# A mixture-of-experts layer on one core: expert rows stored each to a row of its own and summed when the turns end

## What is computed

```python
# T = 768 tokens in layer 0, 512 in layer 1; D = 1024; 64 experts, 8 of them per token
idx = lax.top_k(sel, TOP_K)[1]
wts = jnp.take_along_axis(scores, idx, axis=1)
wts = wts / jnp.sum(wts, axis=-1, keepdims=True) * ROUTED_SCALE
...
def expert_block(...):          # 128 rows of one expert
    xb = h_pad[tok]
    return (jax.nn.silu(xb @ w_eg[e]) * (xb @ w_eu[e])) @ w_ed[e]
routed = jnp.zeros((T + 1, D), h.dtype).at[row_tok].add(y * row_w[:, None])[:T]
shared = (jax.nn.silu(h @ w_sg) * (h @ w_su)) @ w_sd
x = x + gt2 * (routed + shared)
```

## Time and profile before

| | us |
|---|---|
| median of three runs | 3712.47 |
| lowest and highest run | 3701.37, 3768.01 |
| the profiled execution | 3699.51 |
| its span, first to last instruction | 3697.7 |
| layer 0: end of the loop's matmuls to TensorE's next full work | 2049.5 to 2107.8 |
| layer 1: end of the loop's matmuls to the end of the span | 3650 to 3697.7 |

### The profile page before, as it was taken

The page is one execution under the profiler, slowest core; times in us unless marked ns, Lnnn a source line. Parts: engine busy times, 40 slices in busy tenths (PEclk is TensorE's granted clock), DMA queues, the critical chain, the costliest instruction groups (busy, mean ns, idle before and its releaser), DMA issues.

```text
span 3697.7 us, 42657 instructions
## 1 busy us (share of the span) xinstructions
PE 3436.1 (93%) x13496; PEld 2137.5 (58%) x13496; DVE 975.2 (26%) x1798; ACT 755.5 (20%) x1337; POOL 631.0 (17%) x767
## 2 busy tenths in 40 slices
PE   7999999999986999999999499999997799999994
PEld 3468877899653444445444248877764344444442
DVE  2243242122242111111111335233324111111113
ACT  2343242112111111111111235232211111111111
POOL 0000300000023222222222200110003222222222
PEclk9979999999978999999999799979997899999997
DMA  6210211344215999999998510102222899999995
GB/s 241 81 58 7 72 40 58 120 139 146 104 66 218 345 354 348 354 354 355 350 359 297 166 47 1 49 18 69 90 100 71 320 350 343 340 352 344 340 342 149
DMA packets 223706, 735.36 MB, mean 199 GB/s; under 512 B 47842, under 2 KB 96388, under 8 KB 169428
## 3 DMA queue, kind: packets, MB, share of 16 engines
q1 hardware_dynamic: 176356, 601.80, 43.8%
q0 software_dynamic: 47248, 132.13, 14.4%
HBM read 669.89 MB, written 98.31 MB: 208 GB/s over the span
## 4 chain that ended last, share of the span: by engine, by line
PE 90%; DVE 3%; DMA 2%; issue 1%; ACT 1%; POOL 1%; SPq 0%; another core or an unknown queue 0%; POOLq 0%; DVEq 0%; ACTq 0%
PE ps L765 26%; PE ps L792 13%; PE ps L743 8%; PE ps L714 7%; PE ps L721 5%; PE ps L722 5%; PE ps L723 5%; PE ps L899 5%; PE ps L918 4%; PE ps L992 4%; PE ps L820 1%; PE ps L1009 1%; POOL slot_list L1745 1%; PE ps L1004 1%; PE ps L876 1%
## 5 line engine op out<-in xcount | busy, mean ns | idle before, releaser
L765 PE MATMUL ps<-ring,region_q 128*128 128x512 f32 x1120 | 492.2, 592 | 0.0
L1775 POOL DMA_INDIRECT acc<-region_q,idx_out x141 | 226.3, 1605 | 1060.1 <-DVE region_q L1421 1004.0
L743 PEld LDWEIGHTS ps<-con,region_c 128*128 128x128 f32 x1766 | 243.7, 171 | 201.3 <-issue 154.9
L765 PEld LDWEIGHTS ps<-ring,region_q 128*128 128x128 f32 x1120 | 207.9, 191 | 234.4 <-issue 234.4
L743 PE MATMUL ps<-con,region_c 128*128 128x128 f32 x1766 | 281.0, 288 | 51.3 <-DMA region_c<-h_rows,idx_in 28.7
L1057 ACT ACTIVATE region_q<-ps 128x512 f32<-128x512 f32 (+2 forms) x308 | 194.0, 630 | 629.6 <-PE ps L792 416.3
L723 PE MATMUL ps<-region_x_split,ring_split 128*128 128x384 f32 (+2 forms) x800 | 284.4, 356 | 0.0
L765 PE MATMUL ps<-region_k,region_q 128*128 128x512 f32 x576 | 258.2, 602 | 1.7 <-DVE region_q L1389 1.7
L792 PE MATMUL ps<-ring,region_c 128*128 128x512 f32 x560 | 252.0, 593 | 1.0 <-DVE region_c L1401 1.0
L765 PE MATMUL ps<-region_v,region_q 128*128 128x512 f32 x560 | 246.3, 593 | 0.7 <-DVE region_q L1389 0.7
L1073 ACT ACTIVATE region_c<-ps 128x256 f32<-128x256 f32 x141 | 54.1, 384 | 912.7 <-PE ps L765 912.7
(11 more groups left out here) (279 smaller groups left out, 5075.4 us busy)
## 6 DMA issues: line engine op xcount, KB each, us to landing
ring<-in_w_exp_gate SPq DMA_DIRECT2D x70, 1024.0 KB
ring<-in_w_exp_up SPq DMA_DIRECT2D x70, 1024.0 KB
ring<-in_w_exp_down SPq DMA_DIRECT2D x70, 1024.0 KB
ring<-in_w_mod SPq DMA_DIRECT2D x24, 2048.0 KB, 8.1
region_k<-in_w_exp_gate SPq DMA_DIRECT2D x36, 1024.0 KB
region_k<-in_w_exp_up SPq DMA_DIRECT2D x36, 1024.0 KB
region_k<-in_w_exp_down SPq DMA_DIRECT2D x36, 1024.0 KB, 10.4
region_v<-in_w_exp_gate SPq DMA_DIRECT2D x35, 1024.0 KB
```

The costliest lines, as they stand in the source:

```text
L743: last = nc.tensor.transpose(ps[0:t.shape[1], at:at + t.shape[0]], t, ident[0:t.shape[0], 0:t.shape[0]])
L765: last = mm(m_gu[s], xgT[:, s, k, :], wgu[w][:, :, k, :], start=k == 0, stop=k == DK - 1)
L1775: pool.indirect_dma_start(ACC[s], bass.IndirectOffsetOnAxis(ap=idx_out[:, s:s + 1], axis=0), yb[:, s, :], None, compute_op=ALU.add).then_i ...
```

## The change

- Each of a token's eight expert rows gets a place of its own in HBM: `y_rows` has 768 x 8 rows of 1024 numbers, and the list's entry (8 x token + choice) is the row number. The scatter is a plain write; entries past the end are left out by a bounds check.
- The shifted list goes to a tile `rows` of its own, used by the gather; the unshifted `slots` serves the scatter.
- The accumulators, their zeroing, the zero rows of `h_rows` and the stores of the shared expert go. The shared rows (`sd`) are drained by VectorE: times gt2, then added to XT ahead of the loop.
- Behind the loop SP loads, per tile of 128 tokens, a token's eight rows to one partition: rows 0 to 3 as `half_a` (2 MB, a third of `ring`), rows 4 to 7 as `half_b` (2 MB in K, VY or HT). Three tiles fit; the load of tile i waits until tile i - 3 is summed.
- VectorE adds half a pairwise (128x2048, 128x1024). TensorE adds half b by multiplying each row block with the identity and accumulating in PSUM, 8 matmuls of 128x512 per tile. VectorE adds the PSUM sum, multiplies by gt2 and adds to XT. GpSimd adds nothing any more.
- Only the latent tiles are saved to `x_saved` (4 of 6).

```diff
-                add("sd", l, u, drain="act", panel=("shd", l))
+                add("sd", l, u, drain="dve", panel=("shd", l))
...
-    ACC = [nc.dram_tensor(f"acc{i}", [TOK + P, D], F32, kind="Internal").ap() for i in range(2)]
+    Y8 = nc.dram_tensor("y_rows", [TOK * TOPK, D], F32, kind="Internal").ap()
...
+        half_a = [ring[:, 4096 * i:4096 * i + 4096] for i in range(3)]
+        half_b = [w[:, 0:4096] for w in (K, VY, HT)]
...
                 for i, t in enumerate(A):
-                    for a in range(2):
-                        sp.dma_start(comb[i][:, a, :], ACC[a][t * P:t * P + P, :]).then_inc(s_comb[i], 16)
+                    y = Y8[t * P * TOPK:(t + 1) * P * TOPK, :].rearrange("(p j) d -> p (j d)", p=P)
+                    if i >= 3:
+                        sp.wait_ge(b_summed, before + i - 2)
+                        sp.wait_ge(combined, before + i - 2)
+                    sp.dma_start(half_a[i % 3], y[:, 0:4096]).then_inc(s_half_a[i], 16)
+                    sp.dma_start(half_b[i % 3], y[:, 4096:8192]).then_inc(s_half_b[i], 16)
+                    if i >= 3:
+                        save(i - 3)
...
+                    for i in range(len(active(l))):
+                        pe.wait_ge(s_half_b[i], 16 * (l + 1))
+                        if i >= 2:
+                            pe.wait_ge(combined, NT * l + i - 1)
+                        for half in range(2):
+                            for j in range(TOPK // 2):
+                                at = D * j + 512 * half
+                                last = mm(slot[i % 2][:, 512 * half:512 * half + 512], ident, half_b[i % 3][:, at:at + 512],
+                                          start=j == 0, stop=j == TOPK // 2 - 1)
+                        last.then_inc(b_summed, 1)
...
                 for i, t in enumerate(A):
-                    a = comb[i]
-                    dve.wait_ge(summed, i + 1 + (NT if l else 0))
-                    link(tt(a[:, 0, :], a[:, 0, :], BC["gt2", 0 if t >= CT else 1], ALU.mult))
-                    tt(XT[:, t, :], XT[:, t, :], a[:, 0, :], ALU.add).then_inc(combined, 1)
+                    a = half_a[i % 3]
+                    dve.wait_ge(s_half_a[i], 16 * (l + 1))
+                    link(tt(a[:, 0:2 * D], a[:, 0:2 * D], a[:, 2 * D:4 * D], ALU.add))
+                    link(tt(a[:, 0:D], a[:, 0:D], a[:, D:2 * D], ALU.add))
+                    dve.wait_ge(b_summed, NT * l + i + 1)
+                    link(tt(a[:, 0:D], a[:, 0:D], slot[i % 2], ALU.add))
+                    link(tt(a[:, 0:D], a[:, 0:D], BC["gt2", 0 if t >= CT else 1], ALU.mult))
+                    tt(XT[:, t, :], XT[:, t, :], a[:, 0:D], ALU.add).then_inc(combined, 1)
...
+                elif kind == "sd":
...
+                    tt(yb[:, n % 2, :], ps, BC["gt2", 0 if t >= CT else 1], ALU.mult).then_inc(drained["dve"], 1)
+                    dve.wait_ge(drained["dve"], job.count)
+                    link(tt(XT[:, t, :], XT[:, t, :], yb[:, n % 2, :], ALU.add))
...
-                    pool.indirect_dma_start(ACC[s], bass.IndirectOffsetOnAxis(ap=idx_out[:, s:s + 1], axis=0),
-                                            yb[:, s, :], None, compute_op=ALU.add).then_inc(sl[f"scat{s}"], 16)
+                    pool.indirect_dma_start(Y8, bass.IndirectOffsetOnAxis(ap=idx_out[:, s:s + 1], axis=0), yb[:, s, :], None,
+                                            bounds_check=TOK * TOPK - 1, oob_is_err=False).then_inc(sl[f"scat{s}"], 16)
...
-                for i, t in enumerate(A):
-                    a = comb[i]
-                    pool.wait_ge(s_comb[i], 32 * (l + 1))
-                    gp.tensor_tensor(a[:, 0, :], a[:, 0, :], a[:, 1, :], ALU.add).then_inc(summed, 1)
```

More of the change, by code:

```diff
@@ L219, in build @@
           choice, nobody, out):
-    H = nc.dram_tensor("h_rows", [TOK + P, HROW], F32, kind="Internal").ap()
-    ACC = [nc.dram_tensor(f"acc{i}", [TOK + P, D], F32, kind="Internal").ap() for i in range(2)]
+    H = nc.dram_tensor("h_rows", [TOK, HROW], F32, kind="Internal").ap()
+    Y8 = nc.dram_tensor("y_rows", [TOK * TOPK, D], F32, kind="Internal").ap()
     LISTS = [nc.dram_tensor(f"slot_list{l}", [P * LISTN, 1], I32, kind="Internal").ap() for l in range(DEPTH)]
+    SPARE = [nc.dram_tensor(f"spare{s}", [P, 1], I32, kind="Internal").ap() for s in range(2)]
     XS = nc.dram_tensor("x_saved", [TOK, D], F32, kind="Internal").ap()
@@ L354, in build @@
         slots = C[:, 3712:3712 + LISTN].bitcast(I32)
+        rows = C[:, 4096:4096 + LISTN].bitcast(I32)
         xgT = Q[:, 0:2048].rearrange("p (a k s) -> p a k s", a=2, k=DK)
@@ L1248, in _ @@
                     last = copy(hTb[:, n % 2, :], ps[:, 0:DE])
-                elif kind == "sd":
-                    n = active(l).index(a[1])
-                    if n >= 2:
-                        act.wait_ge(s_sh[n % 2], store_no(l, n) - 16)
-                    last = copy(yb[:, n % 2, :], ps)
                 elif kind == "moe":
@@ L1403, in moe @@
                 dve.wait_ge(sl["list_in"], 16)
-                ts(slots, slots, 3, None, ALU.logical_shift_right).then_inc(sl["slots_ready"], 1)
+                ts(rows, slots, 3, None, ALU.logical_shift_right).then_inc(sl["slots_ready"], 1)
                 dve.sem_inc(sl["y_b"], 1)
@@ L1455, in _ @@
             vec.tensor_copy(trib[:], cst("tri"))
-            vec.memset(zero[:], 0.0).then_inc(s_zero, 1)
             for job in jobs:
@@ L1631, in _ @@
                     last = tt(hb[:, n % 2, :], s1[:, n % 2, :], ps[:, DE:2 * DE], ALU.mult)
+                elif kind == "sd":
+                    t = a[1]
+                    n = active(l).index(t)
+                    if n == 0:
+                        for s in range(2 if l < DEPTH - 1 else 1):
+                            after(dve, "bc", l, "gt2", s)
+                    tt(yb[:, n % 2, :], ps, BC["gt2", 0 if t >= CT else 1], ALU.mult).then_inc(drained["dve"], 1)
+                    dve.wait_ge(drained["dve"], job.count)
+                    link(tt(XT[:, t, :], XT[:, t, :], yb[:, n % 2, :], ALU.add))
                 elif kind == "pos":
@@ L1784, in _ @@
                     gather(w, w)
+                if l:
+                    for i in range(NT):
+                        pool.wait_ge(s_half_a[i], 16 * l)
+                        pool.wait_ge(s_half_b[i], 16 * l)
                 for s in range(2):
-                    pool.wait_ge(s_sh[s], store_no(l, len(A) - 2 + s))
-                pool.wait_ge(s_acc1, 16 * (NT + (len(A) if l else 0)))
-                for s in range(2):
-                    pool.dma_start(ACC[s][TOK:TOK + P, :].rearrange("p (a n) -> p a n", a=4), zr).then_inc(sl[f"scat{s}"], 16)
+                    pool.dma_start(SPARE[s], place[:, 0:1]).then_inc(sl[f"scat{s}"], 16)
                 with pool.Fori(0, max_turns(l) // UNROLL) as m:
```

42 lines of the change are left out of this document (16 added, 26 removed).

## The result

The changed kernel took 3826.1 us as the median of four runs (3768.9 to 3893.9), the kernel before beside it 3740.2 us (3701.4 to 3797.6). The ratio is **1.018, interval 1.014 to 1.022**. It compares only the runs of each kernel that lie within 1.5% of its fastest one. Two repeats with more runs gave 1.027 (1.019 to 1.036) and 1.024 (1.015 to 1.034). The change makes the kernel slower by about 2%; on which side of 2% it lies, the three intervals leave open. The median of the first measurement lies above my range, the ratio where the sum had put it.

A forecast was written before the change was run, and what follows sets the result against it. TensorE was taken to pace the loops; the loads behind them cost: 41.7 + 27.4 - 2 x 1.6 - 0.6 + 0.7 = +66.0 us on 3699.5, so 3765.5, with a median allowance 3770 us; range 3748 to 3808 us.

The forecast's parts named there:

- The turns: Expert loops: plain writes replace 141 scatters with addition, TensorE sets the turn of 11.42 us, so 0 change.
- Rivals D and E: D: plain scatter lengthens turns, 3911 us, 4%; E: fewer bytes shorten turns, 3630 us, 4%; at 1 us per turn.
- The last scatter, -1.6 us per layer: End of each loop: plain scatter lands in 4.5 us instead of 6.13, -1.6 us per layer, between -3.1 and 0.
- The streams: Loads behind the loops: 25.17 MB and 16.78 MB at 415 GB/s; stages +41.7 us and +27.4 us.
- rival B: Loads behind the loops run slower, at 346 GB/s; sum +86, 3790 us; 18%.
- The rule weighed: Loads behind the loops: the skill's 358 GB/s per core would make the sum 16 us more; the trace shows 412 to 421.
- The last tile's sum, 8.4 us: Behind the stream: TensorE adds the last tile's half b, 8.4 us, the middle of 6.87 and 9.96 us.
- The lead of 6 us: Loads behind layer 0's loop: tile 4's load may start about 2096, before 2102, so the stream stays full.
- rival C: Behind the loops: TensorE at half clock sets the tiles, 13.3 us each; sum +101, 3805 us; 8%.
- ScalarE's backlog: After the last addition: ScalarE no longer comes to the following code with a backlog, -0.6 us.
- the shared part: Ahead of the loops: VectorE's shared-expert work delays layer 1's list shift, +0.7 us, between 0 and 1.4.
- Rival F: Start of the loops shifts by 10 us either way, to 3760 or 3780 us; 6%.

The follow-up runs named there:

- experiment 5: Kernel before with a plain write in place of the addition in the scatter; 3732.3 us, ratio 1.015 (1.009 to 1.020).
- experiment 4: Changed kernel with GpSimd's loop alone cut from 28 and 24 rounds to 19 and 17; 3774.3 us, ratio 1.023 (1.017 to 1.028).
- experiment 3: Changed kernel with one 128x128 matmul per tile in place of the eight that sum half b; 3757.1 us, ratio 1.016 (1.010 to 1.023).
- experiment 2: Changed kernel loading only half of each token's row data behind the loops, additions and matmuls keeping their shapes; 3769.2 us, ratio 1.022.
- experiment 6: Kernel before with VectorE gating and adding the shared rows ahead of the loop, both accumulators zeroed; 3683.6 us against 3692.0, ratio 1.000 (0.997 to 1.003).
- the combined version: Kernel before with VectorE adding the shared expert ahead of the loop and the two accumulators without GpSimd; 3719.3 us, ratio 1.005; again 3719.2 us, 1.003.
- the changed kernel's third and second: Profiles of the changed kernel run again unedited; third measurement 3813.3 us, ratio 1.024 (1.015 to 1.034), second 3817.7 us, 1.027 (1.019 to 1.036).

## Why the prediction was right, and where it was not

**The turns: right.** 871.8 us with 870.07 us of TensorE, as before, though share and bytes of the queues fell. The plain scatters landed in 9.3 us in the median, not in the 6 of the last one, and still well inside the two turns that cover them. Rivals D and E ask for turns of another length; experiment 5 refutes E a second time.

**The last scatter, -1.6 us per layer: the step failed.** I took 4.5 us to landing; it is 2.82 (experiment 4), just under the 3 to 6 us that I had named as the sign. By that the gain should have been 3.3 us. But the step never asked what was late next. The first load came 0.8 us later in layer 0 and 2.1 earlier in layer 1, since GpSimd's empty loop rounds, hidden behind 6.13 us of landing before, now stand on the path, and its drain behind them is of no fixed length (2.70 us before, 3.92 after in layer 0; 3.83 and 2.12 in layer 1). Sum of both layers -1.3 us instead of -3.2.

**The streams: right that the bytes set them; that the length agrees in layer 0 is luck.** First load's issue to the last byte's signal: predicted 63.0 us, measured 63.4, at 413 to 436 GB/s. In layer 1 predicted 43.9, measured 43.4 (3830.05 to 3873.43). That takes out rival B. But I took 415 GB/s, and tiles come at 428: by that layer 0 needs 61.2 us, which is what experiment 3 shows (61.3). The two late tiles, for which I had no term, give back the 2.2 us. The rule weighed is settled as well. By the 358 GB/s per core that the Trainium skill has in "DMA: Bandwidth & Descriptors", section "Where 436 GB/s comes from", the 25.17 MB alone would have needed 70.3 us. The Trainium skill's other figure, on the same page in the section "Measured (HBM→SBUF, 128 partitions, SWDGE, issued from GpSimd)", is 425 GB/s for 16 MB to one core with the pair's other core idle. The 428 GB/s of this trace agree with that one.

**The last tile's sum, 8.4 us: near in layer 0 (8.65), by other means in layer 1.** I took the middle of two rows, and four profiles show 7.1 to 10.2 us for it in layer 0 (experiment 4); that the first fell on the middle is luck. In layer 1 TensorE needed 7.13, and a wait of 1.0 us for VectorE took the difference. The prediction said that the additions of half a are done while half b still loads; for the last tile of layer 1 that's wrong, because VectorE had the tile before and its norm to finish first. With the three last instructions the stage ends 12.5 us behind the stream in layer 0 and 11.9 in layer 1; predicted 12.1.

**Together:** first load to the end of the last addition 75.9 us against 33.4, +42.5 (predicted +41.7), and 55.2 against 28.6, +26.6 (predicted +27.4). The sums agree, 69.1 and 69.1 us.

**The lead of 6 us: right, rather larger.** The fourth tile's load is issued while the third still streams:

```profile
L691 SPq DMA_DIRECT2D region_k<-y_rows x2: 426/430/435, 2138.4 to 2163.2; - x2
```

2163.2 us against 2171.2, a lead of 8 us; the DMA share in the narrow rows before and after it is 1.01 to 1.02.

**TensorE as the pace (rival C): no.** It waits for every tile of layer 0, and its 16 records take 7.13 us behind one pause of 2.6 us, 8.57 behind the next of 2.65, and 8.63 behind the last of 3.44, never 13.3. With half the bytes VectorE sets the pace at 7.5 us and TensorE follows at 6.9 (experiment 2).

**ScalarE's backlog and the shared part:** between the last addition and TensorE's next matmul 4.38 us instead of 4.58, so -0.2, not -0.6. The +0.7 for the shared part is smaller than what the stretch ahead of the loops varies by, 99 to 111 us in layer 1; experiment 6 bounds it, it doesn't measure it.

**The level:** the sum said +66.0, the stages say +67.9; the difference is the step of the last scatter. The predicted 3770 us fit the ratio and the lower runs of the first measurement (3768.9 to 3775.5), not the medians of 3813 to 3826 us. Rival F named a shift of 10 us ahead of the loops; what really moves is the attention, by 20, 55 and 90 us, and the range had no term for that, though the runs of before, 3701 to 3768 us, showed it. The range's lower end doesn't come out of what it names: 420 GB/s, the scatters at their bound and no allowance take 3770 to 3761 us, not to 3748. Nothing hung on it.

## What to carry to other kernels

Moving an addition from memory writes to the reader multiplies the reader's bytes: here 8 rows instead of 2 sums per token, read when nothing else runs, at a rate that is known beforehand from the same stage. Relief of an engine or a queue inside a loop that TensorE fills to the last hundredth is worth nothing, even when the DMA share says 1.00. And whoever makes the operation that a stage's end waits for faster should name what is late next, down to the loop rounds that a sequencer only counts through.

## What the runs showed of the hardware that I had not expected

**TensorE stays at half clock for 30 to 150 us and more while it is busy all the time.** Some 317 us into layer 1's attention the granted clock falls to 0.50 (1.2 GHz of 2.4), in every profile; in the third of the changed kernel that is 1 us behind a pause of 1.9 us (row from 2440 below). How long it stays there is not the same. First the profile of the combined version that took 3671.0 us, then the changed kernel's third and second:

```profile
2407.00:2437.00 30.00, 30.00 (x102) 23.00 (x101) 8.85 (x20) 6.64 (x16) 0.00 (x0) 0.50 0.00 1
2437.00:2497.00 60.00, 60.00 (x380) 48.10 (x379) 25.87 (x59) 25.10 (x55) 0.00 (x0) 0.98 0.00 1
```

```profile
2440.00:2445.00 5.00, 3.21 (x14) 2.31 (x14) 2.88 (x7) 1.58 (x5) 4.69 (x5) 0.78 0.99 311
2455.20:2530.20 75.00, 75.00 (x250) 56.96 (x250) 19.96 (x43) 15.99 (x36) 0.00 (x0) 0.50 0.00 0
2530.20:2560.20 30.00, 30.00 (x194) 24.37 (x192) 12.54 (x30) 12.70 (x28) 0.00 (x0) 0.98 0.01 2
```

```profile
2463.40:2613.40 150.00, 148.88 (x512) 116.25 (x511) 38.18 (x84) 33.27 (x75) 0.00 (x0) 0.50 0.00 1
```

With no DMA under way and TensorE busy without a gap it goes on at half clock for at least 30, 75 or 150 us, and the attention of layer 1 takes 703, 720 or 756 us by it. All twelve profiles lie at one of these three values (700 to 703, 720 to 723, 756), with the changed combine and without it. Layer 0's attention has the same: from 500 to 700 us the granted clock was 0.56 in the changed kernel's first profile and 0.97 in the kernel before, and its end lay 91 us apart. Such a long spell there was seen in two of the six profiles with the new combine (the other in experiment 4) and in none of the six others, although no instruction of a combine has run by then. In a timed run of the kernel before the mean granted clock was 0.562, and it took 5931 us.

The short value was seen in three of the six profiles with the accumulators of before and in none of the six with the new one. Its lowest timed run, 3744.3 us, lies 20 us under the profile with 719.9 us, as the short value would. Whether the new combine makes long spells likelier, and so costs something beyond the 68 us, is open: no run here holds the attention's timing fixed and changes the combine alone.

**GpSimd's empty loop rounds cost 0.6 us each,** and 2.8 us of them stood on the path in layer 0, 1.6 in layer 1.

**A scatter with addition keeps the DMA engines busy without bytes:** share 1.00 against 0.93 at the same 346 GB/s, 1605 against 1012 ns of GpSimd per scatter, and, for the last one of layer 0's loop, 6.13 against 2.82 us to landing.
